# Who makes the low halves of the weights: VectorE and GpSimd, or VectorE alone

## What is computed

```python
for i in range(DEPTH):                      # mixer 0: swa_sink, mixer 1: dilated
    x = x + mixer(rms_norm(x, norm)) @ w_out
return rms_norm(x, final_norm)
# swa_sink: q, k, v, gate = split(h @ w_in); rope on the first 16 of 64 columns of q, k
#   4 key heads, window 128, a sink logit per head in the denominator; o * silu(gate)
# dilated: three patterns (window, dilation) = (128,1), (512,4), (2048,16), each with its
#   own q, k, v; the three outputs are weighted by softmax of their log-denominators;
#   sum * silu(gate)
```

## Time and profile before

| | us |
|---|---|
| median of 3 runs | 1317.85 |
| lowest and highest | 1316.67, 1317.91 |
| profiled execution, whole | 1317.86 |
| its span, first to last instruction | 1316.1 |
| TensorE busy | 1272.8 (97%) |
| VectorE busy | 767.8 (58%) |
| ScalarE busy | 643.5 (49%) |
| GpSimd busy | 367.1 (28%) |

### The profile page before, as it was taken

How to read it: one execution, slowest core, us unless ns; L and a number is a source line. 1 busy time by engine, 2 the same in 40 slices (tenths; PEclk the granted TensorE clock), 3 DMA queues, 4 the chain that set the end, 5 groups by cost and what they waited for, 6 DMA issues and landing times.

```text
span 1316.1 us, 24587 instructions
## 1 busy us (share of the span) xinstructions
PE 1272.8 (97%) x8714; PEld 1184.7 (90%) x8714; DVE 767.8 (58%) x2345; ACT 643.5 (49%) x1777; POOL 367.1 (28%) x427
## 2 busy tenths in 40 slices
PE   5999999999999999999999999999999999989997
PEld 4998998987799999899989999899999899977997
DVE  5745453545672545666546766556765466767925
ACT  6445453544651535555446554446454465554312
POOL 2311151240311031212214922216722219510010
PEclk9999999999999999999999999999999999999999
DMA  5101022031445211101112311212310213214623
GB/s 201 40 17 49 25 65 73 19 96 49 161 145 199 97 33 45 39 25 23 53 49 67 83 57 35 64 37 75 107 31 18 64 48 97 71 38 133 200 98 128
DMA packets 101223, 97.29 MB, mean 74 GB/s; under 512 B 30704, under 2 KB 87536, under 8 KB 101104
## 3 DMA queue, kind: packets, MB, share of 16 engines
q1 hardware_dynamic: 101104, 95.73, 24.4%
HBM read 79.46 MB, written 16.25 MB: 73 GB/s over the span
## 4 chain that ended last, share of the span: by engine, by line
PE 66%; DVE 4%; ACT 1%; DMA 1%; issue 1%; SPq 0%; POOL 0%; DVEq 0%; ACTq 0%
PE j_bank L1145 46%; PE o_bank L1288 6%; PE t_bank L1267 5%; PE s_bank L1254 3%; PE j_bank L1232 2%; PE s_bank L1256 2%; PE o_bank L1145 1%; PE t_bank L1145 1%; DMA w_raw<-in_w_qkv 1%; PE s_bank L1145 1%; ACT probs L1387 1%; DVE xr L1803 0%; DVE ht_lo L1816 0%; DVE xr L1868 0%; DVE xr L1805 0%
## 5 line engine op out<-in xcount | busy, mean ns | idle before, releaser
L1145 PE MATMUL j_bank<-w_hi,ht_hi 128*128 128x384 f32 (+1 forms) x1312 | 444.8, 339 | 4.4 <-ACT v L1401 2.4
L1145 PE MATMUL j_bank<-w_lo,ht_hi 128*128 128x384 f32 (+1 forms) x1312 | 432.8, 330 | 0.0
L1145 PE MATMUL j_bank<-w_hi,ht_lo 128*128 128x384 f32 (+1 forms) x1312 | 432.7, 330 | 0.0
L1145 PEld LDWEIGHTS j_bank<-w_hi,ht_hi 128*128 128x128 f32 x1312 | 248.5, 189 | 15.9 <-issue 8.7
L1041 POOL TENSOR_TENSOR w_lo<-w_raw,w_hi 128x768 fp32r<-128x768 f32 (+1 forms) x60 | 102.5, 1709 | 561.7 <-ACT w_hi L1378 561.2
L1387 ACT ACTIVATE probs<-probs,stat 128x256 f32<-128x256 f32 (+1 forms) x512 | 231.0, 453 | 38.6 <-DVE stat L1644 36.7
L1145 PEld LDWEIGHTS j_bank<-w_lo,ht_hi 128*128 128x128 f32 x1312 | 248.8, 190 | 0.0
L1145 PEld LDWEIGHTS j_bank<-w_hi,ht_lo 128*128 128x128 f32 x1312 | 248.4, 189 | 0.0
L777 ACT COPY probs_t<-t_bank 128x256 f32<-128x256 f32 (+1 forms) x128 | 58.0, 453 | 296.6 <-PE o_bank L1288 291.0
L1378 ACT ACTIVATE w_hi<-w_raw 128x768 fp32r<-128x768 f32 (+1 forms) x120 | 88.3, 763 | 78.7 <-PE j_bank L1145 43.6
L1636 DVE CUSTOM_DVE_ANT_0 probs<-s_bank,masks 128x256 f32<-128x256 f32 x224 | 86.1, 421 | 57.0 <-PE t_bank L1267 56.2
(11 more groups left out here) (170 smaller groups left out, 1856.8 us busy)
## 6 DMA issues: line engine op xcount, KB each, us to landing
w_raw<-in_w_qkv SPq DMA_DIRECT2D x64, 384.0 KB, 3.4
coef<-coef_dram SPq DMA_DIRECT2D x96, 128.0 KB, 2.9
w_raw<-in_w_gate SPq DMA_DIRECT2D x32, 256.0 KB, 3.3
mix_dram<-xr SPq DMA_DIRECT2D x12, 512.0 KB, 3.9
w_raw<-in_w_out SPq DMA_DIRECT2D x16, 384.0 KB, 3.9
qk<-mix_dram SPq DMA_DIRECT2D x12, 512.0 KB, 4.0
xr<-in_x SPq DMA_DIRECT2D x8, 512.0 KB, 7.0
out<-xr SPq DMA_DIRECT2D x7, 512.0 KB, 2.7
```

What stands on the lines that cost most here:

```text
L1145: last = pe.matmul(to, a(x_, kt), b(y_, kt), start=(start and kt == kts[0] and x_ == y_), stop=(stop and kt == kts[-1] and x_ == 1))
```

## The change

VectorE makes the low halves of all quarters, at the places where it makes the even ones, one after the other. GpSimd's calls of its own `w_lo` are gone. The two counting semaphores become one, and SyncE and TensorE wait on it with counts in quarters.

```diff
-        w_lo_done = {"v": sem("w_lo_v"), "p": sem("w_lo_p")}
+        w_lo_done = sem("w_lo_done")
...
-                    sp.wait_ge(w_lo_done["vp"[q % 2]], m // 2)
+                    sp.wait_ge(w_lo_done, m - 1)
...
-            def w_lo(quarters):
-                for n, q in quarters:
-                    if q % 2 == 1:
-                        pool.wait_ge(w_hi_done, 4 * n + q + 1)
-                        pool.tensor_tensor(quarter(n, q, 1), raw_quarter(n, q), quarter(n, q, 0).bitcast(F32),
-                                           ALU.subtract).then_inc(w_lo_done["p"], 1)
...
-                w_lo([(JOB["qkv", steps[1].t], 2), (JOB["qkv", steps[1].t], 3)])
...
-                        w_lo(SLOT_SPLIT.get((s.t, slot), []))
-                        if slot == UNITS - 1:
-                            w_lo(SPLIT_BEHIND.get(s.t, []))
...
-                w_lo(END_SPLIT[layer])
...
-                pe.wait_ge(w_lo_done["vp"[q % 2]], 2 * JOB[job] + q // 2 + 1)
+                pe.wait_ge(w_lo_done, 4 * JOB[job] + q + 1)
...
             def w_lo(quarters):
                 for n, q in quarters:
-                    if q % 2 == 0:
-                        dve.wait_ge(w_hi_done, 4 * n + q + 1)
-                        dve.tensor_tensor(quarter(n, q, 1), raw_quarter(n, q), quarter(n, q, 0).bitcast(F32),
-                                          ALU.subtract).then_inc(w_lo_done["v"], 1)
+                    dve.wait_ge(w_hi_done, 4 * n + q + 1)
+                    dve.tensor_tensor(quarter(n, q, 1), raw_quarter(n, q), quarter(n, q, 0).bitcast(F32),
+                                      ALU.subtract).then_inc(w_lo_done, 1)
```

More of the change, by code:

```diff
@@ L1091, in link @@
                 pool.wait_ge(mixed, value)
-            w_lo(splits_of("start") + splits_of("start, second half") + splits_of("start, next job"))
             for layer in (0, 1):
```

## The result

The changed kernel takes 1322.56 us in the median of 5 runs (1322.1 to 1324.81), the kernel before 1317.68 beside it (1316.67 to 1317.91): a ratio of 1.004, with a 95% interval of 1.0027 to 1.0053. That is 4.9 us slower, where +2.0 us was forecast. It lies inside the range of 1316 to 1326, but beyond the 0.2% that the forecast gave the most chance; the range reached so far only for rival (a), which did not come, so that the time lies inside it is in part luck. On another chip, later, the ratio was 1.0048 (1.0036 to 1.006).

What follows compares the result with a forecast made beforehand. TensorE's own stream was taken as the bound, busy 1272.8 of 1316.1 us. The terms 0.85 + 0.6 + 0.85 - 0.6 + 0.3 gave +2.0 us on 1317.85, so 1319.9 us, range 1316.0 to 1326.0.

Steps and rivals of the forecast that it cites:

- rival (a): Inside the steps: VectorE's queue becomes late, splits delay masks and so TensorE's bank; 6.3 us more, 1326; chance 0.27.
- Bound and cover: Whole kernel: TensorE's stream bounds; VectorE or GpSimd changes move only the 43 us in which TensorE is not busy.
- VectorE's sum: VectorE's busy time: 767.8 + 51.6 - 10, some 810 us, 61% of the span.
- Places 1 to 3: Chains without slack: start's first piece +0.85 us, start's second half +0.6, turn between the layers +0.85.
- Place 4: End of layer 1: odd split lengthens the chain, but TensorE's later waits shrink; -0.6 us, bounds -1.5 and +0.3.
- swallowed by the wait: End of layer 1: the chain's added 0.95 us vanishes in TensorE's wait for the next job's quarters.
- SyncE's loads: SyncE's queue: next weight load stands behind the odd split, ending 0.9 us sooner or 1.8 later; taken as zero.
- The price named for lost cover: SyncE's weight loads: if quarters were not first used tens of us later, 1.8 us once per load.
- Place 5: Inside the steps: split pairs and single splits mostly hidden; +0.3 us together, bounds -1 and +6.
- the masks behind the pairs: Between steps: seven of fourteen split pairs push the next step's masks by 0.9 us; idle up to 2.86 us behind.
- The contention that goes: VectorE and GpSimd splits no longer meet: 10 us of VectorE back; as a rival, outweighs added instructions, 1315, chance 0.07.
- Sum: Whole kernel: 0.85 + 0.6 + 0.85 - 0.6 + 0.3 = +2.0 us, 1319.9 us, 0.15% slower.

Runs made afterwards that it cites:

- e1: Kernel before, with VectorE making only the seven odd low halves of the start and the turn between the layers: 1321.09 us, ratio 1.0020.
- e10: Kernel before, with VectorE making only the three odd low halves of the end of layer 1: 1318.39 us, ratio 1.0006.
- e2: Kernel before, with VectorE making only quarter 3 of jobs 15, 19 and 23 (slot 11 of steps 6, 9, 12): 1320.49 us, ratio 1.0015.
- e4: Kernel before, with SyncE issuing slot 11's two weight loads ahead of the store of the values: 1317.23 us, ratio 0.9990.
- e9: Kernel before, with VectorE making 47 of the 60 odd low halves, those inside the steps and in layer 0's output projection: 1320.27 us, ratio 1.0022.
- e7: Kernel before, with slot 11's loads ahead of the store and VectorE making the last job's two odd low halves: 1317.01 us, ratio 0.9993.
- e6: Kernel before, with VectorE making only the last job's two odd low halves: 1317.41 us, ratio 0.9997.
- e5: Changed kernel, but GpSimd keeps the ten odd low halves of start, turn and slot 11 of steps 6, 9, 12: 1322.69 us, ratio 1.0029 to kernel before.
- e12: The same kernel as e5, run again on another chip: 1320.17 us, ratio 1.0026 to the kernel before.

## Why the prediction was right or wrong

**Bound and cover.** That it is TensorE's idle time that moves held nearly: 3.9 of the 4.6 us are idle time. VectorE's sum held within 7 us.

**Places 1 to 3: right.** +0.85, +0.6 and +0.85 were forecast; 0.85, 0.57 and 0.85 came, with tiles ending at 25.09 (25.0 forecast) and the two transposes 0.90 and 1.42 us late (0.85 and 1.45). The rows were read where VectorE's program order, GpSimd's start and TensorE's wait met in one chain, and e1 bears the three out alone.

**Place 4: wrong in sign.** The chain came as forecast (+0.87 for 0.95). The step that failed is that it would be "swallowed by the wait". I took the moment at which TensorE gets the next job's quarters as fixed. But the loads land behind that of the final norm's weights, which SyncE issues 0.2 us ahead of the last mixer tile, when the same chain lets it. So when the chain shifts, this load, the tile, the landing and the wait shift together, and only the part at the last quarter is won: the 0.27 us for GpSimd's split. That makes +0.87 - 0.27 = +0.6 us instead of -0.6. In thirteen of fourteen traces ScalarE gets those quarters 6.4 to 6.8 us after the tile's start, whichever engine split, and in the last after 7.0. The net of the two last stretches is +0.07 in one trace of the changed kernel, +0.65 in the other and +0.35 in e10. In the first of these luck helps: the last stretch is 0.21 to 0.36 us shorter in e1, e2 and e4 too, where nothing was changed.

**SyncE's loads: the step that cost most.** "I take zero; the cover is that quarters made singly are first used tens of us after" names the wrong user. TensorE does use them late; but ScalarE, strictly in order, stands at its high half until the load is there, and the gate copy stands behind it. The 0.27 us of idle time ahead of ScalarE's high half at 657.66 already told that this load had no slack. The price named for lost cover, 1.8 us per load, was too high: the store is 0.49 us late, and with what the landing adds the wait grew by 2.7 us over three places in the first trace, 0.9 in the second.

**Place 5 and rival (a).** Place 5 was put too low. +0.3 us was forecast, and e9, in which the moved splits lie inside the steps and in layer 0's output projection, costs 2.9 (1.6 to 4.3). Of these, 1.6 us are the gate wait of steps 6 and 9, behind loads that land later; why they do stays open, and so does the rest. But it is not the masks behind the pairs: between the steps of the difference the traces run in parallel, and the 6.3 us of rival (a) didn't come. The contention that goes is worth nothing that can be seen; the one stretch where it seemed so (0.7 us at 745 to 760) is as short in kernels that keep GpSimd's splits there. That the two engines hold each other up beside the mixing too shows in a row:

```profile
902.76 3.28 POOL L1073 TENSOR_TENSOR xr<-xr,coef 128x512 f32<-128x512 f32 x2 [3.70 <-DMA coef<-coef_dram]
...
903.00 1.89 DVE L1585 TENSOR_TENSOR w_lo<-w_raw,w_hi 128x768 fp32r<-128x768 f32 x1 [2.87 <-ACT w_hi L1361]
```

It is the longest of the 120, twice the 0.95 us of one alone, and TensorE passes it without a wait. At slot 11 it was the queue behind the splits in which the time went.

**Sum.** 2.27 at places 1 to 3, 0.6 at place 4 and 1.8 at slot 11 (the mean of 2.7 and 0.9) make 4.7 us, against the 4.9 between the medians of the first measurement and 6.2 of the second. The +2.0 was right at the front by its working; of the 2.9 us it lacked, 1.2 are place 4, and most of the rest is slot 11, which the mean of two traces so unlike sizes only roughly.

No version ran measurably better than the kernel before with its loads first (e4, 0.1% faster). e7, which has VectorE make the last two as well, has a median 0.2 us lower, on another chip, and a ratio that cannot be told from it.

## What to carry to other kernels

When a step moves to another engine, follow not only who uses its result but every queue in order behind it: here a copy, a store behind the copy, a load behind the store, and a third engine that stands for the load with an unrelated copy behind. Idle time of 0.3 us that ends with a DMA, on an engine that runs strictly in order ahead of something TensorE needs, is such a chain with no slack left. And ask of a wait that is to swallow a delay whether what ends it is itself released by the delayed work, and of a load that is to be issued sooner what stands ahead of it in its queue.

## What the runs showed of the hardware

**A load behind others lands by them.** At the end of layer 1 the first weight load landed 0.62 to 0.75 us behind the load issued ahead of it, in fourteen of fourteen traces, while the distance between the two issues was 2.07 us in nine of them and 3.16 or 3.17 in five.

**Landing varies more than the engines do.** With issue at the same distance from TensorE's piece, the second of the two loads at slot 11 of step 6 reached ScalarE 5.12 us after the first's issue (before), 5.13 (e10), 5.19 (e1) and 5.81 (e6), with nothing changed there. Each such place adds up to 0.7 us of chance to one execution, more than most terms of the sum.

**A code packet among the loads.** In all seven traces in which VectorE makes the odd low halves inside the steps, the DMA view shows one packet of instructions on queue 14 within the 6 us behind the issue at slot 11, in all three steps; in none of the other seven. This is e9, from 654 to 657 us:

```profile
q1 hardware_dynamic: 1060, 0.91, 90.7%
q14 instruction: 1, 0.01, 0.6%
```

In e5, e9 and e12 it comes 2.0 to 3.5 us after the issue at steps 6 and 9, amid the loads, and the second high half starts 5.93 to 6.45 us after the issue; with no such packet there, and the loads behind the store as in the kernel before, 4.90 to 5.85. In the two traces of the changed kernel it comes at the issue itself, and the figures there are 4.83 to 6.10. That the packet is the cause was not tested. It takes 0.6% of the engines' time in these 3 us, which speaks against it. By the Trainium skill (Runtime: NRT & Kernel Launch, "Instruction fetch mechanics") crossing to the next block of code is mostly hidden; that is said of the engine that runs the code, and no run here shows what it does to other transfers. What makes the second load 0.8 us late in e5, e9 and e12 stays open.
